# One core, two layers of a hybrid backbone: norms by 32 rows, first weights loaded a stage ahead, and the second mixer stretch with pair 1 first

## The reference

```python
def _rmsnorm(x, gain):
    y = xf * lax.rsqrt(jnp.mean(xf * xf, axis=-1, keepdims=True) + NORM_EPS)
    return (y * gain).astype(x.dtype)
def _swiglu(h, w_in, w_out):
    gate, up = jnp.split(h @ w_in, 2, axis=-1)
    return (jax.nn.silu(gate) * up) @ w_out
def _adaln(cond, w, b):
    mod = jax.nn.silu(cond) @ w + b
    return mod.reshape(cond.shape[0], N_MOD, D_MODEL)
```

## Time and profile before

| stage | from to | long | PE busy | DVE busy | clock |
|---|---|---|---|---|---|
| first | 0 to 37.6 | 37.6 | 17.0 | 4.8 | 0.99 |
| ffn1, layer 0 | to 354.7 | 317.1 | 301.4 | 122.1 | 0.97 |
| mix_in, layer 0 | to 510.1 | 155.4 | 136.9 | 88.8 | 0.94 |
| gla_and_pair, layer 0 | to 638.7 | 128.6 | 105.2 | 67.5 | 0.82 |
| two_pairs, layer 0 | to 773.4 | 134.7 | 113.5 | 80.4 | 0.93 |
| ffn2, layer 0 | to 1120.4 | 347.0 | 321.5 | 143.7 | 0.94 |
| ffn1, layer 1 | to 1416.8 | 296.4 | 281.1 | 121.7 | 0.97 |
| mix_in, layer 1 | to 1571.4 | 154.6 | 137.0 | 88.8 | 0.94 |
| gla_and_pair, layer 1 | to 1703.1 | 131.7 | 100.8 | 67.4 | 0.79 |
| two_pairs, layer 1 | to 1833.8 | 130.7 | 110.3 | 80.4 | 0.88 |
| ffn2, layer 1 | to 2178.0 | 344.2 | 317.1 | 143.7 | 0.96 |
| last | to 2194.1 | 16.1 | 0.0 | 8.6 | 0.50 |

### The profile page before, as it was taken

One profiled execution on the slowest core, in us unless ns is written; L12 is line 12 of the kernel. 1 busy time (PEld: TensorE's weight loads), 2 busy tenths in 40 slices (PEclk: granted clock), 3 DMA queues, 4 the chain that ended last, 5 costly groups with the idle time before them and its releaser, 6 DMA issues. The chain is left out here.

```text
span 2194.1 us, 37567 instructions
## 1 busy us (share of the span) xinstructions
PE 1941.8 (88%) x16146; PEld 1757.4 (80%) x16146; DVE 1017.9 (46%) x1509; ACT 725.2 (33%) x1043; POOL 31.0 (1%) x62
## 2 busy tenths in 40 slices
PE   4999997997988968999979999799878796799996
PEld 1989996984655768999969999788657495799996
DVE  3333334655546554343344443464454755544434
ACT  3322324334242224332243332242431423433321
POOL 0000000001000000000000000000000100000000
PEclk8999998997979988999989999999878798899998
DMA  7665343314527032332323333332230502233232
GB/s 276 216 226 194 103 132 135 114 58 144 170 82 213 23 134 77 134 118 103 130 102 132 128 110 118 126 137 82 79 94 5 156 4 99 81 131 129 103 123 76
DMA packets 72612, 263.21 MB, mean 120 GB/s; under 512 B 9632, under 2 KB 10656, under 8 KB 56224
## 3 DMA queue, kind: packets, MB, share of 16 engines
q1 hardware_dynamic: 72480, 261.27, 35.0%
HBM read 259.08 MB, written 2.16 MB: 119 GB/s over the span
## 5 line engine op out<-in xcount | busy, mean ns | idle before, releaser
L149 PE MATMUL ps<-h_head,w_head 128*128 128x384 f32 x1952 | 672.0, 344 | 98.1 <-DVE h_rest L439 60.9
L149 PE MATMUL ps<-h_rest,w_head 128*128 128x384 f32 x1952 | 661.4, 339 | 0.0
L149 PE MATMUL ps<-h_head,w_rest 128*128 128x384 f32 x1952 | 661.2, 339 | 0.0
L358 DVE TENSOR_TENSOR w_rest<-w_raw,w_head 128x2048 fp32r<-128x2048 f32 (+1 forms) x186 | 383.7, 2063 | 347.7 <-ACT w_head L352 347.5
L149 PEld LDWEIGHTS ps<-h_head,w_head 128*128 128x128 f32 x1952 | 372.0, 191 | 135.4 <-DVE w_rest L358 83.7
L149 PEld LDWEIGHTS ps<-h_rest,w_head 128*128 128x128 f32 x1952 | 373.1, 191 | 0.2
L149 PEld LDWEIGHTS ps<-h_head,w_rest 128*128 128x128 f32 x1952 | 372.9, 191 | 0.0
L352 ACT ACTIVATE w_head<-w_raw 128x2048 fp32r<-128x2048 f32 (+1 forms) x186 | 321.0, 1726 | 156.1 <-PE ps L149 138.9
L149 PE MATMUL ps<-gu_head,w_head 128*128 128x384 f32 x704 | 237.0, 337 | 9.6 <-DVE gu_rest L602 7.2
L149 PE MATMUL ps<-gu_head,w_rest 128*128 128x384 f32 x704 | 237.0, 337 | 0.0
L149 PE MATMUL ps<-gu_rest,w_head 128*128 128x384 f32 x704 | 236.8, 336 | 0.0
(11 more groups left out here) (279 smaller groups left out, 1746.1 us busy)
## 6 DMA issues: line engine op xcount, KB each, us to landing
w_raw<-in_w_in SPq DMA_DIRECT2D x88, 1024.0 KB, 4.8
ada_raw<-in_ada_w SPq DMA_DIRECT2D x64, 1024.0 KB, 6.6
w_raw<-in_w_out SPq DMA_DIRECT2D x64, 704.0 KB, 4.1
w_raw<-in_mix_in SPq DMA_DIRECT2D x26, 1024.0 KB, 4.8
square<-in_ada_w SPq DMA_DIRECT2D x8, 1024.0 KB, 6.1
w_raw<-in_mix_out SPq DMA_DIRECT2D x8, 1024.0 KB, 4.9
hyena_const<-in_hconst SPq DMA_DIRECT2D x2, 1792.0 KB, 10.8
x<-in_x_in SPq DMA_DIRECT2D x1, 1536.0 KB, 11.8
```

The source lines that it names most:

```text
L149: return nc.tensor.matmul(out, lhsT, rhs, start=start, stop=stop)
L358: nc.vector.tensor_tensor(self.LO[:, j % 2, 0:cols], self.RAW[:, j % 2, 0:cols], self.HI[:, j % 2, 0:cols].bitcast(F32), ALU.subtract).the ...
```

## The change

1. `w_raw` is one buffer for the whole program. The last issues of each stage's SyncE stream are the first two units of the next (`load_ahead`): weights of ffn1, mix_in or mix_out, or units 0 and 1 of the adaptive norm's set. Where a dense stage follows a dense one, the stage ahead also splits the next first unit (`split_next_head`, `split_next_rest`); in the others it is split in two halves at the head of the stage. The first unit's blocks run with kt outside.
2. The short norm: `total` lays the three groups of 128 tokens on three strips of 32 rows; root and reciprocal are on 96x128; `spread_rows` brings them back over 128 rows with three matmuls. VectorE multiplies x by the scale and by the spread value in one instruction for each of the two token segments, ScalarE writes h_head with the shift, VectorE h_rest. The last square goes to TensorE without VectorE's addition. `load_root_table` takes a root of one element at the end of the stage ahead.
3. In two_pairs, pair A's chain stands in the streams beside B's inverse, B's chain alone at the end, and units 1,5 to 1,7 of the adaptive norm's second set behind B's inverse. (Layer 1 has one set there, layer 0 two.)
4. The last stage has the short norm, one instruction a tile, and the output in four DMAs. The loop over layers is written out.

```diff
+        RAW = right(stack, "w_raw", [128, 2, 2048])
+        NEXT = [stack.enter_context(nc.semaphore(f"next{i}")) for i in range(2)]
+            def load_next(self, sp, units, sources):
+                for u, (src, cols) in enumerate(sources):
+                    sp.wait_ge(self.rest_ready, units - 1 + u)
+                    load_ahead(sp, (units + u) % 2, cols, src)
+            def split_next_head(self, act, units):
+                act.wait_ge(NEXT[0], ahead[0])
+                act.wait_ge(self.used, units - 1)
+                for h in range(2):
+                    self.head((slice(None), 0, slice(h * 1024, h * 1024 + 1024))).then_inc(self.next_head, 1)
...
+        def total(src, start, stop):
+            for j in range(3):
+                last = mm(bank(7, 128, 32 * j, 32 * j + 32), cst("ones", 0, 32), src[:, 128 * j:128 * j + 128], start, stop)
+        def spread_rows(inverse):
+            for j in range(3):
+                last = mm(bank(4 + j, 128), cst("ones", 0, 128, 32 * j, 32 * j + 1), inverse[32 * j:32 * j + 1, 0:128])
...
+                nc.vector.reciprocal(self.RSTD[ROOTS, 0:128], self.STD[ROOTS, 0:128]).then_inc(self.xn_done, 1)
+                dve.wait_ge(self.spread_done, 1)
+                def scaled(dt):
+                    for s, (a, b) in enumerate(SEGS):
+                        last = nc.vector.scalar_tensor_tensor(by_128(self.SQ[:, dt, a:b]), by_128(X[:, dt, a:b]), AFF[:, self.i, dt, s:s + 1],
+                                                              spread_at(a, b), ALU.mult, ALU.mult)
...
-                for dt in range(KT - 3, KT):
+                for dt in range(KT):
+                    scaled(dt)
+                    if split and 1 <= dt <= 2:
+                        split(dt - 1)
+                    if dt >= 2:
+                        rest(dt - 2)
+                for dt in range(KT - 2, KT):
                     rest(dt)
...
+                def _(act):
+                    W.count_first(act, W.head_ready)
                     N.root(act)
-                    N.heads(act, lambda: W.split_head(act, 0, 2, 0, 2048))
+                    N.heads(act)
                     for n, u in enumerate(UNITS):
                         if n + 1 < N_MIX:
                             W.split_head(act, n + 1, 2, 0, 2048)
```

More of the change, by code:

```diff
@@ L187, in __init__ @@
                 self.slots, self.banks, self.sets, self.at = slots, banks, len(banks), 0
-                if raw is None:
-                    own = sb(scope, "ada_raw", [128, slots, ADA_J * ADA_W])
-                    raw = [own[:, s, :] for s in range(slots)]
-                self.RAW = raw
+                self.loaded = list(ahead) if raw is None else None
+                self.RAW = [RAW[:, s, :] for s in range(slots)] if raw is None else raw
                 self.rows = self.sets if kept is None else kept
@@ L286, in _ @@
                     ADA.row(act, 0)
+                    load_root_table()
                 @block.vector
@@ L2491, in _, with weights, ada_units @@
                     B.dve_dev_inverse(dve)
-                    A.dve_out(dve)
                     B.dve_out(dve)
             zero_semaphores()
-        first_stage()
-        def layer(lay, sets, first_sets, ada_first, ada_to):
-            ffn_stage(lay, 0, w1_in, w1_out, None, first_sets)
+        def weights(w, at, cols):
+            return [(rows(w, at + u), cols) for u in range(2)]
+        def ada_units(first):
+            return [(ada_slice(first, u), None) for u in range(2)]
+        ADA_SETS = (4, 2)
@@ new lines, in build @@
+        ADA_AT = (ADA_FIRST, N_ADA + ADA_FIRST - 2)
+        ADA_TO = (0, MOD_TILES - 2 * ADA_T)
+        dense = ExitStack()
+        buffers = split_buffers(dense)
+        first_stage(weights(w1_in, 0, 2048))
+        for lay in range(DEPTH):
+            mixes = [(rows(mix_in, lay * N_MIX + u), 2048) for u in MIX_UNITS[0:2]]
+            ffn_stage(lay, 0, w1_in, w1_out, None, buffers, lay > 0, mixes, 0 if lay else 2)
+            sets_each, ada_first, ada_to = ADA_SETS[lay] // 2, ADA_AT[lay], ADA_TO[lay]
+            ada_second = ada_first + sets_each * ADA_J
```

571 lines of the change are left out of this document (334 added, 237 removed).

## The result

The changed kernel took 2166.82 us as the median (2164.82 to 2173.24), the kernel before 2192.79 beside it: a ratio of 0.9887, with a 95% interval from 0.9861 to 0.9912. That is 26 us less. The time is inside the forecast range of 2132 to 2172, but the gain is little more than half of the 44.8 that the sum gave. The profiled execution's span went from 2194.1 to 2164.8, 29.3 less.

The account below looks back on a forecast made before the run. TensorE was taken as nearly full, with time to gain where it waits for h_rest and adaptive-norm weights. Heads and loads -56.8, reordered stretch +8, clock +4 sum to -44.8 us: about 2150 us median, range 2132 to 2172.

Parts of the forecast that it names:

- the heads: Stage starts: shorter norm and weights split early make first units come out sooner; mix_in 22.8 to 16.9 us, 11.6 for two.
- the second unit's split: In stage heads: ScalarE and VectorE split the second unit's weights last, at S+16.9, making this the new bound.
- the sum of squares and ffn2: Both ffn2: mix_out's first unit saves 12 us, the norm inside 9; the total stays at its old price, 1.65.
- Weights of the adaptive norm one stage ahead: First mixer stretch: loading both first units a stage ahead removes TensorE's starting wait, 5.5 us per layer, 11 together.
- the reordered stretch: Second mixer stretch: A's chain beside B's inverse, B's alone, costs +3 and +5 us by layer, plus +4 for clock.
- The start of A's inverse: Second mixer stretch, layer 0: some 2.4 us earlier, as two of B's grams no longer stand before it.
- nothing more: Second mixer stretch: loading weights ahead gains nothing, since products already come later in TensorE's queue than their data.
- The free order: Rival, second mixer stretch: A's chain fills TensorE holes, up to 8 us less a layer, 2135 median; chance 0.17.
- Low clock in the heads: Rival: first units run at 1.2 GHz, a head gives 2 us, not 5.8; total 2165 to 2180; chance 0.18.
- the loads were not what was late: Rival: slower scaled pieces from PSUM delay the second unit's split, 2.5 us a head, 17 in all, 2168; chance 0.06.
- The slower kernel: Rival: the clock stays low beyond the heads, 8.0 us per unit at half clock, slower than before; chance 0.02.
- lone chains run low: Second mixer stretch: a chain running alone gets a lower clock; wholly so 6.2 us a layer, a third taken, +4 together.

Follow-up runs that it names:

- e7: The changed kernel with the norm's sum, root and reciprocal on 128x384 again, without spreading matmuls: 2175.99 us.
- e6: The changed kernel with the old order of two_pairs and three slots for the adaptive norm's weights there: 2136.14 us.
- e8: The changed kernel without the root of one element ahead, so the table loads in front of the root again: 2163.89 us.
- e11: The changed kernel with units 1,5 to 1,7 of the adaptive norm moved into B's lone chain: 2161.84 us.
- e2: The kernel before with only the new order of two_pairs added: 2221.20 us, ratio 1.0119.
- e9: e1 with units 0 and 1 of the adaptive norm's set for gla_and_pair loaded at that stage's own head again: 2144.18 us.
- e1: The changed kernel with the old order of two_pairs in the TensorE, ScalarE and VectorE streams: 2141.44 us, ratio 0.9762.
- e4: The changed kernel with the first adaptive-norm set's products at their old places in TensorE's stream of two_pairs: 2161.81 us.
- e5: The changed kernel, new order kept, with three slots instead of two for the adaptive norm's weights in two_pairs: 2157.15 us.
- e12: The changed kernel, new order kept, with the edits of e4, e5 and e11 together: 2157.07 us, ratio 0.9833.
- e3: The changed kernel with pair A's reciprocal and outputs moved later on VectorE, behind B's first x: 2163.94 us.

## Why the prediction was right, and where its sum was off

**Right: the heads.** The reciprocal took 0.95, as worked out from the earlier trace rows; the spread 0.80 at the low clock; a pair of scaled pieces 0.73 and a tile 1.31 (forecast 1.37). The first silu of ffn1 in layer 1 is out 18.5 into the stage, forecast 18.7. The mechanism was right but for one point: the second unit's split is not the new bound. TensorE waits for it only in the two ffn2, 0.80 and 0.38 us; in mix_in and ffn1 its last wait is the one for the first h_rest (2.90 in mix_in), and from there its own products fill the time. Mix_in gave more than forecast since I let everything wait for the second unit: the first unit was out at 15.2 in layer 0, and TensorE went on with the second at 15.8.

**Too low: the sum of squares and ffn2** (-26.7, forecast -21). The timeline of ffn2 in layer 0 of the changed kernel:

```profile
792.52 1.39 DVE L587 SCALAR_TENSOR_TENSOR x<-ps,gate,x 128x128 f32<-128x128 f32 x4 [3.43 <-PE ps L154]
...
820.72 0.65 PE L154 MATMUL ps<-rstd,const 128*32 128x128 f32 x6 [3.28 <-DVE rstd L521]
...
836.97 0.49 ACT L677 ACTIVATE silu<-ps 128x384 f32<-128x384 f32 x1 [0.32 <-PE ps L154]
```

Mix_out's first unit is done at 12.9 (20.3 before), and from there to the silu it is 44.5, not 52.2. The products that are three strips took 0.65 where 1.65 stood in the earlier trace rows. Both stand at the low clock (0.50). That is 2.5 times, and the Trainium skill's 2.38 for three column tiles (TensorE: Matmul & The Clock Gate, "Part 3: Packing small matmuls — row/col tiling") is close to it. The last square now has such a group of its own, and both together take 1.08. I had left the total at its old price, as the prediction said. By e7 this and the shorter root and reciprocal are some 9 us over the whole kernel.

**The step that failed in gla_and_pair (forecast -11, measured -2.0)** is "Weights of the adaptive norm one stage ahead": I took the wait that goes away for the time that is saved. The wait did go. The waits at later units stayed about as they were (3.62 and 2.09 now, 3.13 and 2.00 before, in layer 0), and units 0 to 9 are done 5.3 us earlier (545.14 in a stage from 500.5, against 560.02 from 510.1). What took it back is the clock of what follows, up to the next products. Before, in the changed kernel, and in e6:

```profile
560.02:581.58 21.56, 20.78 (x452) 16.96 (x450) 10.14 (x38) 6.07 (x10) 0.00 (x0) 0.94 0.31 97
545.14:572.40 27.26, 26.52 (x450) 21.13 (x451) 9.24 (x35) 6.08 (x10) 0.00 (x0) 0.72 0.21 69
545.66:567.48 21.82, 20.19 (x452) 16.63 (x450) 9.87 (x36) 6.08 (x10) 0.00 (x0) 0.99 0.31 97
```

The same products took 5.7 us longer in the changed kernel's profile than before. That is not fixed by the change: e6, e8 and e11 have the same streams in this stage and stood there at 0.98 to 1.00 (stages of 125.0 to 125.6), the eight others with these streams at 0.68 to 0.72 (127.5 to 130.6). Compared at like clock, the loads ahead are worth some 3 to 4 us in layer 0: 125.0 to 125.6 against 128.6 and 129.7 (before, e2) with the higher clock in that stretch, and 127.5 to 130.6 against 132.2 (e9) with the lower. In layer 1 the eleven stages are 126.5 to 129.8 long, the three without the loads ahead 131.4 to 131.9. So the term is worth about 7 and not 11, by my estimate from these lengths, and the measured 2.0 is so far below it by the luck of one profile. Where the other 4 go is seen in layer 1: TensorE's idle time fell by 5.6, as forecast, but its busy time for the same instructions rose by 3.4 (100.8 to 104.2).

**The term that was mis-sized most is the reordered stretch: +12 forecast, +25.3 measured, 25 to 27 by e1 and e2.** By its steps, in layer 0:
- The start of A's inverse: forecast 2.4 earlier, measured 4.6 later. This was the wrong sign. I had looked at VectorE's grams, not at where units 0 and 1 now stand in TensorE's stream. e4 puts them back and gets the 4.5. The 7 us between 2.4 earlier and 4.6 later are the largest part of the 10.6 by which layer 0 was off.
- To B's first x: 66.4, forecast 63.3. The 2.98 wait for unit 1,7 is in it; it is issued only when unit 1,5 has been used, and that is now at 740. In layer 1 it is 58.4, forecast 58.1 (41.0 before, 15.1, and 2 for the wait behind A's outputs). That is near, though the wait itself was 4.23 and not 2: it was fully exposed, and the rest of the sum came out 1.9 shorter.
- B's chain: 18.9 and 19.6, forecast 18.2 with its clock. Near. At the low clock throughout it is 23.5 and 23.6 (e5, e12).
- The tail: 8.4 and 7.8, forecast 9.0. The one reciprocal saved is real.

Layer 1 was also off on the other side. There the measured +9.7 hides a gain: e1 shows that, order aside, this stage became 4.5 shorter, so the order's own price in layer 1 is 140.4 - 126.2 = 14.2. The "nothing more" for loads in the second stretch was wrong by up to 4.5 there. In layer 0 it was wrong the other way, with the order: 5.89 of waiting at unit 2.

The two layers lose the time in different ways. In layer 0 TensorE's busy time for the same instructions rose by 10.5 (113.5 to 124.0, the clock from 0.93 to 0.85) and its idle time by 5.1; in layer 1 busy time rose by 0.9 and idle time by 8.8.

What the chains lost is plain in two windows. Interleaved: 22.3 us with 22.1 of work at clock 1.00 (e1). Alone in the changed kernel, layers 1 and 0: 19.6 us with 14.8 of work and 18.9 with 14.2 for **one** chain. From the start of A's inverse to the end of the chains TensorE was idle for 0.2 of 70.5 us before; after, it is idle for 8.6 of 85.3.

**The rivals.** The free order (0.17) fell with e1; its sum was also off by one, since 12 less 8 a layer is -4 and not -3. Low clock in the heads (0.18) did not happen: in mix_in of layer 0 the first products stood at 0.50 for 3.7 us (358.50 to 362.2) and the rest of the first unit at full clock, and the dense stages as a whole stand at 0.94 to 0.97. That the loads were not what was late (0.06) needed a pair of scaled pieces at 1.0; it took 0.73. The slower kernel (0.02) fell too. What was costed at nothing, the table load ahead, does show at the tail (e8), but by no more than it saves.

That lone chains run low is half true. In the sixteen lone chains without products in them (nine profiles) the mean clock was 0.50 in three (e3's and e5's layer 0, e12's layer 1) and 0.60 to 0.81 in the others, never 1.00; the ten interleaved ones (five profiles) all stood at 1.00, and so did e12's layer 0, where products filled the lone chain. The rule of the Trainium skill (TensorE: Matmul & The Clock Gate, "HAM oscillation — how this bites in real kernels") speaks of bursts between waits for DMA that are longer than the bursts, and I stretched it to a chain with hops of 0.4 to 0.6 us. Its "every time" is not what these runs show: after 4.23 us of waiting TensorE came back at the lower clock (1.12 for 16 products in layer 1 of the changed kernel), after 3.23 at the full one (0.68 in e11).

## What to carry to other kernels

A load that is issued a stage ahead is worth at most the wait that it removes: look at what the engine does next and at which clock, and at when the first slot is handed back to the ring. A chain of small dependent products was cheapest here beside a second such chain; to run them one after the other saved a reciprocal at the end and paid with idle hops and a lower clock, and in layer 0 most of that came back once its weights were there in time and other products stood inside the lone chain (e12). When a change has several parts, price the moved ones by the idle time of the engine that is full now: here there was none to gain. And where a stage's clock varies from run to run, compare it over several profiles of the same instructions before a difference is put down to a change.

## What was not expected of the hardware

The same chain of small products took 17.8 us at a clock of 1.00, with two products of another kind in it, and 23.6 at 0.50 without, in one and the same profile (e12). The clock of such stretches differs from run to run with the same instructions. One stretch of gla_and_pair took 21.8 us at 0.99 in e6 and 27.3 at 0.72 in the changed kernel, and with it the stage's length spread over 5.6 us in eleven profiles. The four runs of e3 spread over 26 us, and the slower ones had the lower mean clock.
